# A two-layer hybrid decoder trunk: gathered experts against all experts on TensorE

## The chip, the cores and the metric

The kernel runs on one core of a Trainium2 chip. The metric is device time in microseconds of one execution, as the median of several runs. One execution of the kernel before was also recorded by the hardware profiler; all rows shown here come from it.

## The reference, cut to what matters

256 tokens of width 1024 go through two layers in float32. Layer 0 mixes tokens with a complex diagonal state-space model (S5), a GELU and a gated linear unit; layer 1 with causal attention over three dilated windows (16 heads of 64). After each mixer comes a PEER channel mixer: a retrieval among 16384 single-neuron experts.

```python
def peer_ffn(h, w_q, sub_keys, u_tab, v_tab):        # u_tab, v_tab: (16384, 1024) per layer
    q = (h @ w_q).reshape(bsz, seq, 8, 2, 128)
    s = einsum('blhpe,hpne->blhpn', q, sub_keys)      # 8 heads x 2 halves x 128 keys
    s_top, i_top = top_k(s, 16)
    cand = s_top[..., 0, :, None] + s_top[..., 1, None, :]
    best, pos = top_k(cand, 16)                       # 16 of 256 sums
    idx = first_key * 128 + second_key                # expert number
    gate = softmax(best)
    act = einsum('cd,ckd->ck', h, u_tab[idx])         # 8 x 16 = 128 experts per token
    return einsum('ck,ckd->cd', gate * gelu(act), v_tab[idx])

# layer: x += mixer(rms_norm(x)); x += peer_ffn(rms_norm(x)); at the end rms_norm(x)
# mixer of layer 1: qkv = h @ w_qkv (1024 x 9216), rope, 3 window groups, @ w_o
```

Only 128 of the 16384 experts have a gate that isn't zero for a token, and a gate depends on the expert's first key i and second key j.

## The kernel before, in words

Tokens are two chunks of 128, one token per partition. The work has four phases: layer 0 chunk 0, layer 0 chunk 1, layer 1 chunk 0, layer 1 chunk 1. A phase is a mixer for one chunk, its norms, the query projection (`peer_scores`, L528) and the top 16 (`top_k_part`, L1493, in four quarters of two heads). The experts of one phase are computed under the mixer of the next.

Expert work goes through the class `Gather` (L319). Each phase has 128 steps. At a step GpSimd issues one indirect DMA (L1233) that brings, for 32 tokens x 4 experts, 128 rows of u and v side by side (1 MB) into one of 8 slots of `ringmem`. VectorE multiplies u with the token's h and sums (L1262), ScalarE takes the GELU (L820) and builds a 128 x 32 matrix `S` with the gated activations (L816, L825), and TensorE adds the v rows into the tokens' sums in PSUM banks 0 and 1 (L448), two steps at once. All engines place these steps into their own order of the other work with `g.at(phase, n)`; `QKV_AT`, `HEADS_AT`, `S5_AT` and the like (L343 to L357) say at which pair of steps each part of a mixer comes. `spread_block` (L455) copies h four times for the layout of the gathers; ScalarE also rearranges row numbers and gates (L898).

Weights come over SP's queue in 2 MB items into a double buffer `wt` (L373, L389): GLU, query, Q/K/V and output weights. In layer 1 each chunk reads all 18 items of `w_qkv` for itself. `project` (L505) does 8 matmuls of 512 moving columns for an item (L509); `project_turned` (L513) does 32 of 128 columns (L523), so that the query comes out turned. Each matmul is float32.

Within a phase TensorE, VectorE and ScalarE each run in program order; what they wait for are semaphores counted by item, step and event.

Of the kernel before, what the change touches and what calls it, by code (L numbers as in the profile page):

```python
# [9 lines left out]
U32 = mybir.dt.uint32  # L30
# [4 lines left out]
P = 128  # L35
# [3 lines left out]
KT = D // P  # L39
EPS = 1e-6  # L40
# [12 lines left out]
RING = 8  # L53
PAIRS_G = STEPS // 2
QUAD = 4
TG = P // QUAD
QUADS = STEPS // QUAD
QPQ = QUADS // QUARTERS
# [9 lines left out]
GLU, WQ0, ITEMS0 = 0, 4, 8  # L68
WT0 = 2
QKV, WO, WQ1, ITEMS1 = 0, 18, 20, 24  # L70


C_ID, C_RAMP, C_IOTA, C_COS, C_SIN, C_REP, C_ALL = 0, 128, 256, 272, 400, 528, 656
M_AT = (0, NG * P)
M_ALL = NG * P + NG * 2 * P
A_WORDS = 15872


TopK = namedtuple("TopK", "stop itop itopf best pos posi posj posij posf gsum grec found gex S2 cand eq")


def item(layer, c, i):


    if layer == 0:
        return i - WQ0 if c == 0 else WT0 + i
    return WT0 + ITEMS0 + ITEMS1 * c + i


def norm_event(layer, c, ffn):  # L90

    return 4 * layer + 2 * c + ffn


def build(nc, x, gains, lam, b_in, c_out, d_skip, w_glu, w_qkv, w_o, w_q, keys, experts, consts,
          masks, out):
    ctx = ExitStack()
    with ctx:
# [6 lines left out]

        X = sb("X", [P, NC, D])
        H = sb("H", [P, D])
        Hrep = sb("Hrep", [P, QUAD, D])
        hT = sb("hT", [P, KT, P])
        gT = sb("gT", [P, KT, P])  # L110
        gain = sb("gain", [P, D])
        wt = sb("wt", [P, 2, KT, BLOCK])
        ringmem = sb("ringmem", [P, RING * 2 * D])
        area = sb("area", [P, A_WORDS])
        con = sb("con", [P, C_ALL])
        sel = sb("sel", [P, 2, QSTEPS])
        lay = sb("lay", [P, NC, 2, QUAD, QUADS])
        rows = lay[:, :, 0].bitcast(U32)
        dots = sb("dots", [P, 2, 2])
        gelus = sb("gelus", [P, 2, 2])  # L120
        S = sb("S", [P, 2, 2, TG])
# [15 lines left out]
        rep = con[:, C_REP:C_REP + P]  # L137
        own = con[:, C_REP:C_REP + TG]

# [16 lines left out]
        cosT = view(area, 0, PAIRS, P)  # L156
        sinT = view(area, 4096, PAIRS, P)
        WB = view(area, 8192, KT, 2, P)
        CW = view(area, 10240, PAIRS, 2, 32)
        T1, T2, T3, P1, P2, P3, P4 = [view(area, 12288 + 512 * i, PPT, P) for i in range(7)]  # L160
        mag, z0re, z0im = [zs[:, i, :] for i in range(3)]
        hflat = Hrep[:, :, :].rearrange("p j d -> p (j d)")
        T4 = P1
        MG = [view(area, 12288 + 512 * i, PPT, P) for i in (4, 5)]
        ZR, ZI = [view(hflat, 512 * i, PPT, P) for i in range(2)]
        Q1, Q2, Q3, Q4 = [view(hflat, 2048 + 512 * i, PPT, P) for i in range(4)]
        sig = view(area, 12288, D)

        craw = view(ringmem, 0, 2, PAIRS, GH)
        tmpc = view(ringmem, 1024, 2, PAIRS, GH)  # L170
        small = view(ringmem, 2048, 20, PAIRS)
        wq_ring = [view(ringmem, 4096 * i, KT, BLOCK) for i in (2, 3)]
        wglu = [wt[:, 1]] + [view(ringmem, 4096 * i, KT, BLOCK) for i in (1, 2, 3)]
# [4 lines left out]
        gflat = gT[:, :, :].rearrange("p k t -> p (k t)")  # L178
        keysT = view(area, 12288, HP, NKEYS)
        qT = view(area, 14336, 2, QHP, P)  # L180
        qs = sb("qs", [P, 512])

        def top_k_places(small, big):
            best, pos, posi, posj = [view(small, 192 + 32 * i, QH, TOPK) for i in range(4)]
            return TopK(stop=view(small, 0, QHP, TOPK), itop=view(small, 64, QHP, TOPK).bitcast(U32),
                        itopf=view(small, 128, QHP, TOPK), best=best, pos=pos.bitcast(U32),
                        posi=posi.bitcast(U32), posj=posj.bitcast(U32),
                        posij=view(small, 256, 2, QSTEPS).bitcast(U32),
                        posf=view(small, 320, 2 * QSTEPS), gsum=view(small, 416, QH),
                        grec=view(small, 418, QH), found=view(small, 420, 2, QSTEPS),  # L190
                        gex=view(small, 384, QH, TOPK), S2=view(big, 0, QHP, NKEYS),
                        cand=view(big, 512, QH, TOPK * TOPK), eq=big)

        late = wt[:, 1].rearrange("p k n -> p (k n)")
        late_scores = [view(late, 1024 + 512 * i, QHP, NKEYS) for i in range(2)]
        places = top_k_places(qs, gflat)
        late_places = top_k_places(late[:, 2048:2560], late)

        def top_k_at(ph, i):

            return late_places if ph == 0 and i >= 2 else places

        MS = view(qs, 0, PPT, P)


        K0 = view(area, 0, NG, 8, P)
        V0 = view(area, 3072, NG, D)
        K1 = view(area, 6144, NG, 4, P)
        V1 = view(area, 7680, NG, BLOCK)
        QT = view(area, 9216, NG, 4, P)  # L210
        RA = view(area, 10752, BLOCK)
        RB = view(area, 11264, BLOCK)
        RR = [view(area, 11776 + BLOCK * i, BLOCK) for i in range(2)]
        SS = [view(area, 10752 + 768 * i, 768) for i in range(2)]
        PT = [view(area, 12288 + 768 * i, 768) for i in range(2)]
        mask = view(area, 13824, 2 * NG * P)
# [1545 lines left out]
```

## Time and profile before

| | |
|---|---|
| median of 3 runs | 1752.47 us (1749.7 to 1760.04) |
| span of the profiled execution | 1755.3 us; no other time of it was taken |
| mean granted TensorE clock | 0.868 of full speed |
| PE, PEld busy | 1285.1 us (73%), 544.9 us (31%) |
| DVE, ACT, POOL busy | 1120.6 us (64%), 677.5 us (39%), 616.7 us (35%) |
| moved by DMA | 685.81 MB, mean 391 GB/s |

PE is TensorE's matmuls, PEld its weight loads, DVE VectorE, ACT ScalarE, POOL GpSimd, SP the queue engine. Busy time is the union of the instructions' records. Matmuls are pipelined and their ends are modelled, so the time from one group's start to the next one's is a better price than a record's length. PEclk is the clock that was granted, as a share of 2.4 GHz. "Idle before" names what released an engine that had stood idle.

### The profile page before, as it was taken

The numbers are of one execution on the slowest core, as the hardware profiler recorded it, in microseconds if no ns is written. First come the engines' busy times: TensorE is split into PE (matmuls) and PEld (weight loads), VectorE is DVE, ScalarE is ACT, GpSimd is POOL, SyncE is SP. The second block draws the span as 40 slices with busy tenths as digits, with TensorE's granted clock in tenths as the row PEclk, the third lists the DMA queues.
The fourth block names the chain that finished last, engine by engine and source line by source line (L and its number), as shares of the span: only waits on it lengthen the run. The fifth ranks groups of instructions, "written<-read, shape, count | busy, mean of one in ns | idle before, by whom it ended". The sixth has DMA issues, their size and how long they took to land.

```text
span 1755.3 us, 17565 instructions
## 1 busy us (share of the span) xinstructions
PE 1285.1 (73%) x5714; PEld 544.9 (31%) x5714; DVE 1120.6 (64%) x2526; ACT 677.5 (39%) x2033; POOL 616.7 (35%) x557
## 2 busy tenths in 40 slices
PE   3876565666969968997788895899886975545454
PEld 2463111222713313333244331543451810000000
DVE  8967999863568765436347966553554567676544
ACT  7643232322243257128134333821652233233222
POOL 4213444442242243224223323332442144444442
PEclk9988877688989979998899998999997976786878
DMA  8099999999999999999999999999999899999997
GB/s 332 7 367 378 380 366 390 392 407 422 424 420 423 424 422 421 426 422 421 423 414 418 415 423 411 381 386 424 422 379 423 332 333 411 418 418 412 420 421 299
DMA packets 86636, 685.81 MB, mean 391 GB/s; under 512 B 9872, under 2 KB 10256, under 8 KB 12176
## 3 DMA queue, kind: packets, MB, share of 16 engines
q0 software_dynamic: 73728, 536.90, 74.9%
q1 hardware_dynamic: 12816, 147.79, 20.3%
q8 instruction: 45, 0.74, 0.2%
q14 instruction: 47, 0.39, 0.1%
HBM read 683.60 MB, written 1.05 MB: 390 GB/s over the span
## 4 chain that ended last, share of the span: by engine, by line
PE 34%; DMA 33%; DVE 19%; ACT 6%; issue 5%; POOL 2%; SPq 0%; POOLq 0%; ACTq 0%; DVEq 0%
DMA ringmem<-experts,lay 24%; PE ps L509 11%; PE ps L448 11%; PE ps L523 6%; DMA wt<-w_qkv 6%; DVE ringmem L1262 6%; POOL ringmem L1233 2%; DMA wt<-w_o 2%; ACT S L825 1%; ACT lay L898 1%; PE ps L727 1%; PE ps L702 1%; PE ps L461 1%; PE ps L713 1%; DMA wt<-w_glu 1%
## 5 line engine op out<-in xcount | busy, mean ns | idle before, releaser
L1233 POOL DMA_INDIRECT ringmem<-experts,lay x512 | 585.3, 1143 | 1062.4 <-PE ps L448 932.0
L448 PE MATMUL ps<-ringmem,S 128*32 128x512 f32 x2048 | 618.2, 753 | 368.3 <-ACT S L825 364.3
L1262 DVE CUSTOM_DVE_ANT_0 ringmem<-ringmem,Hrep 128x1024 f32<-128x1024 f32 x384 | 461.1, 1224 | 260.4 <-DMA ringmem<-experts,lay 257.9
L448 PEld LDWEIGHTS ps<-ringmem,S 128*32 128x32 f32 x2048 | 112.6, 126 | 761.7 <-ACT S L825 516.4
L820 ACT ACTIVATE gelus<-dots 128x2 f32<-128x2 f32 x256 | 51.5, 201 | 628.7 <-DVE dots L1262 624.0
L509 PE MATMUL ps<-wt,hT 128*128 128x512 f32 x576 | 256.2, 598 | 13.8 <-DMA wt<-w_qkv 13.8
L1262 DVE CUSTOM_DVE_ANT_0 ringmem<-ringmem,area 128x1024 f32<-128x1024 f32 x128 | 155.6, 1225 | 110.6 <-DMA ringmem<-experts,lay 110.0
L509 PEld LDWEIGHTS ps<-wt,hT 128*128 128x128 f32 x576 | 106.7, 190 | 164.1 <-issue 153.8
L816 ACT ACTIVATE S<-con,lay 128x32 f32<-128x32 f32 x512 | 134.6, 311 | 39.7 <-PE ps L448 39.1
L825 ACT ACTIVATE S<-S,gelus 128x32 f32<-128x32 f32 x512 | 136.8, 314 | 24.6 <-ACT gelus L820 1.1
L523 PEld LDWEIGHTS ps<-hT,wt 128*128 128x128 f32 x896 | 104.4, 197 | 12.1 <-issue 11.9
L523 PE MATMUL ps<-hT,wt 128*128 128x128 f32 x896 | 107.3, 282 | 0.0
L509 PE MATMUL ps<-wt,gT 128*128 128x512 f32 x128 | 63.2, 652 | 12.6 <-DMA wt<-w_o 10.5
L820 ACT ACT_TABLE_LOAD x55 | 70.6, 1283 | 1.0
L898 ACT COPY lay<-sel 32x16 f32<-32x16 f32 (+1 forms) x272 | 54.4, 200 | 18.8 <-DVE sel L1586 15.8
L1090 ACT COPY area<-ps 128x512 f32<-128x512 f32 x12 | 7.0, 586 | 135.3 <-PE ps L509 135.3
L1607 DVE TENSOR_TENSOR area<-ps,con 128x512 f32<-128x512 f32 x24 | 16.6, 690 | 65.9 <-PE ps L509 56.7
L1622 DVE CUSTOM_DVE_ANT_0 area<-ps,area 128x384 f32<-128x384 f32 (+1 forms) x32 | 24.2, 757 | 46.2 <-PE ps L702 46.2
L1510 DVE MAX8 qs<-ps 128x8 f32<-128x128 f32 x56 | 12.6, 285 | 62.0 <-PE ps L546 47.4
L1262 DVE DVE_READ_ACCUMULATOR2_ANT dots<- 128x1 f32 x512 | 42.1, 82 | 0.0
L509 PEld LDWEIGHTS ps<-wt,gT 128*128 128x128 f32 x128 | 26.1, 209 | 50.8 <-issue 34.6
L1065 ACT ACT_TABLE_LOAD x32 | 41.1, 1283 | 0.6
(234 smaller groups left out, 1237.1 us busy)
## 6 DMA issues: line engine op xcount, KB each, us to landing
wt<-w_qkv SPq DMA_DIRECT2D x36, 2048.0 KB, 11.6
wt<-w_q SPq DMA_DIRECT2D x14, 2048.0 KB, 11.3
wt<-w_glu SPq DMA_DIRECT2D x5, 2048.0 KB, 11.9
ringmem<-experts,lay POOLq DMA_INDIRECT x512, 12.5
wt<-w_o SPq DMA_DIRECT2D x4, 2048.0 KB, 14.4
ringmem<-w_glu SPq DMA_DIRECT2D x3, 2048.0 KB, 21.5
gain<-gains SPq DMA_DIRECT2D x9, 512.0 KB, 11.1
area<-keys SPq DMA_DIRECT2D x4, 1024.0 KB, 9.6
```

The lines of the kernel that those rows point to most:

```text
L448: last = pe.matmul(ps[TG * t:TG * (t + 1), half, :], S[:, u % 2, i, :], ring[:, (2 * u + i) % RING, D + half * 512:D + (half + 1) * 512], ...
L461: pe.matmul(ps[:, bank, :], rep[rows_j, :], H[rows_j, half * 512:(half + 1) * 512], start=True, stop=True, skip_group_check=True).then_inc ...
L509: last = pe.matmul(ps[:, bank, :], act[:, k, :], wt[:, n % 2, k, :], start=(k == 0), stop=(k == KT - 1))
L523: last = pe.matmul(ps[:, bank, m * P:(m + 1) * P], w[:, k, m * P:(m + 1) * P], hT[:, k, :], start=(k == 0 and m == parts[0]), stop=(k == K ...
L816: last = act.activation(S[:, u % 2, i, :], own, ACT.Copy, scale=lay[:, phase % NC, 1, j - 1 + i, n:n + 1])
L820: act.activation(gelus[:, u % 2, :], dots[:, u % 2, :], ACT.Gelu_apprx_tanh).then_inc(gelu_ready, 1)
L825: last = act.activation(S[:, u % 2, i, :], S[:, u % 2, i, :], ACT.Copy, scale=gelus[:, u % 2, i:i + 1])
L898: last = act.copy(lay[TG * r:TG * (r + 1), ph % NC, :, j, n:n + width], sel[TG * j:TG * (j + 1), :, at + width * r:at + width * (r + 1)])
L1065: act.activation(SS[u % 2][:, 0:n], SS[u % 2][:, 0:n], ACT.Exp, bias=nmx[:, u:u + 1], scale=DH ** -0.5, accum_out=den[:, u:u + 1]).then_in ...
L1233: pool.indirect_dma_start(ring[:, s % RING, :], None, experts[phase // NC], bass.IndirectOffsetOnAxis(ap=rows[:, phase % NC, j, n:n + 1], ...
L1262: last = v.tensor_tensor_reduce(ring[:, i, 0:D], ring[:, i, 0:D], hrep(phase, j), 1.0, 0.0, ALU.mult, ALU.add, dots[:, b, second:second + 1])
L1622: v.tensor_tensor_reduce(SS[u % 2][:, 0:n], banks(2, 4)[:, at:at + n], mask[:, 0:n], 1.0, NEG, ALU.add, ALU.max, mx[:, u:u + 1]).then_inc( ...
```

## The change

- No gathers. The u and v tables are read whole, in loads of 1 MB: one load holds, for two first keys i, the 128 experts of each. `u_load` multiplies all 128 experts of a first key with the tokens of one chunk (128 columns) or both (256 columns), ScalarE's GELU writes the result to `acts` (seen as `W[second key, chunk, first key, token]`). `v_load` multiplies `W` of one or both chunks with the v rows and adds into PSUM.
- Gates as a matrix. For each token, `second_keys` (VectorE) makes a 128 x 128 matrix with the gate at each chosen expert's second key, one row per chosen expert; `first_keys` (GpSimd) one with a 1 at its first key. TensorE multiplies the two (`gates`), four tokens a group, and `apply_gates` (VectorE) multiplies `W` with the result.
- One stream. SP issues all loads in the order of `stream_order()` into four slots of 1 MB (`RING`), each when the load four before it is used: 448 loads in all. Both chunks share a load of query, Q/K/V and output weights. Chunk two lags: the first `AHEAD` u loads of a layer are used for chunk 0 alone while chunk 1's mixer goes on, and read again for chunk 1; v the same.
- Query projection for both chunks at once (256 columns). Attention's heads run for both chunks after half of the Q/K/V items. GpSimd takes one of four products of chunk 1's scan.

The core of the diff (semaphore and buffer declarations left out; unchanged steps as well):

```diff
-RING = 8
-QUAD = 4
-QKV, WO, WQ1, ITEMS1 = 0, 18, 20, 24
+RING = 4
+LOADS = NKEYS // 2
+LOAD_WORDS = 2 * D
+AHEAD = (34, 30)
+GROUP = 4
+GROUPS_C = P // GROUP
+def stream_order():
+    order = []
+    for layer in range(LAYERS):
+        ahead = AHEAD[layer]
+        if layer == 1:
+            order += [("qkv", t, half) for t in range(QITEMS) for half in range(2)]
+            order += [("wo", i, half) for i in range(2) for half in range(2)]
+            order += [("u", 1, 0, n) for n in range(ahead)]
+        else:
+            order += [("u", 0, 0, n) for n in range(S5_LOADS)]
+            order += [("glu", k) for k in range(KT)]
+            order += [("u", 0, 0, n) for n in range(S5_LOADS, ahead)]
+        order += [("wq", layer, n) for n in range(HP // 2)]
+        order += [("u", layer, 0, n) for n in range(ahead, LOADS)]
+        order += [("u", layer, 1, n) for n in range(ahead)]
+        order += [("v", layer, 0, n) for n in range(LOADS)]
+        order += [("v", layer, 1, n) for n in range(ahead)]
+    return order
+S5_STEP_LOADS = (3, 3, 3, 3, 3, 3, 3, 3)
...
+            for n, key in enumerate(ORDER):
...
+                if n == 0:
+                    sp.wait_ge(cw_ready, 4)
+                if n == 2:
+                    sp.wait_ge(y_ready, KT)
+                    sp.wait_ge(z0_ready, KT)
+                if n >= RING:
+                    sp.wait_ge(used, n - RING + 1)
+                sp.dma_start(ring[:, n % RING, :], source(key)).then_inc(landed[n % RING], 16)
...
+            def u_load(layer, turn_of, n):
+                key = ("u", layer, turn_of, n)
+                at = load(*key)
+                bank = 6 + EVACUATED[key] % 2
+                if EVACUATED[key] >= 2:
+                    pe.wait_ge(evacuated, EVACUATED[key] - 1)
+                alone = turn_of == 1 or n < AHEAD[layer]
+                cols = slice(P * turn_of, P * (turn_of + 1)) if alone else slice(0, SEQ)
+                width = P if alone else SEQ
+                for b in range(2):
+                    for k in range(KT):
+                        last = pe.matmul(ps[:, bank, b * width:(b + 1) * width],
+                                         at[:, D * b + P * k:D * b + P * (k + 1)], hF[:, k, cols],
+                                         start=(k == 0), stop=(k == KT - 1), skip_group_check=True)
+                last.then_inc(used, 1)
+            def v_load(layer, turn_of, n):
+                at = load("v", layer, turn_of, n)
+                chunks = (turn_of,) if turn_of or n < AHEAD[layer] else (0, 1)
+                for b in range(2):
+                    i = 2 * n + b
+                    for c in chunks:
...
+                        for half in range(2):
+                            last = pe.matmul(ps[:, 2 * c + half, :], W[:, c, i, :],
+                                             at[:, D * b + BLOCK * half:D * b + BLOCK * (half + 1)],
+                                             start=first, stop=end, skip_group_check=True)
+                last.then_inc(used, 1)
+            def gates(layer, c, g):
+                q = gate_group(layer, c, g)
+                pe.wait_ge(hot_j_ready, q + 1)
+                pe.wait_ge(hot_i_ready, q + 1)
+                if g >= 2:
+                    pe.wait_ge(gated, q - 1)
+                for r in range(GROUP):
+                    last = pe.matmul(ps[:, 4 + q % 2, r * P:(r + 1) * P], hot_j[q % 2][:, r, :],
+                                     hot_i[q % 2][:, r, :], start=True, stop=True, skip_group_check=True)
+                last.then_inc(gates_done, 1)
+            def experts(layer):
+                ahead = AHEAD[layer]
+                all_scores(layer)
+                for n in range(ahead, LOADS):
+                    u_load(layer, 0, n)
+                turn_sel(layer, 0)
+                for n in range(ahead):
+                    u_load(layer, 1, n)
+                    for g in groups_behind(n, ahead):
+                        gates(layer, 0, g)
+                turn_sel(layer, 1)
+                pe.wait_ge(gated, gate_group(layer, 0, GROUPS_C - 1) + 1)
+                for n in range(ahead):
+                    v_load(layer, 0, n)
+                    for g in groups_behind(n, ahead):
+                        gates(layer, 1, g)
+                pe.wait_ge(gated, gate_group(layer, 1, GROUPS_C - 1) + 1)
+                for n in range(ahead, LOADS):
+                    v_load(layer, 0, n)
...
+            def project(t, c):
...
+                for half in range(2):
+                    w = load("qkv", t, half)
+                    for k in range(4):
+                        last = pe.matmul(ps[:, project_bank(t, c), :], hF[:, 4 * half + k, P * c:P * (c + 1)],
+                                         w[:, BLOCK * k:BLOCK * (k + 1)], start=(half == 0 and k == 0),
+                                         stop=(half == 1 and k == 3), skip_group_check=True)
+                    if c == 1:
+                        last.then_inc(used, 1)
...
+            def first_keys(layer, c):                      # GpSimd
+                for g in range(GROUPS_C):
...
+                    for r in range(GROUP):
+                        last = pool.tensor_scalar(hot_i[q % 2][:, r, :], count, selT[:, c, 0, t:t + 1], None,
+                                                  ALU.is_equal)
+                    last.then_inc(hot_i_ready, 1)
...
+            def second_keys(layer, c, g):                  # VectorE
...
+                for r in range(GROUP):
+                    last = v.tensor_scalar(hot_j[q % 2][:, r, :], count, selT[:, c, 1, t:t + 1],
+                                           selT[:, c, 2, t:t + 1], ALU.is_equal, ALU.mult)
+                last.then_inc(hot_j_ready, 1)
+            def apply_gates(layer, c, g):
...
+                at = W[:, c, :, GROUP * g:GROUP * (g + 1)]
+                v.tensor_tensor(at, at, ps[:, 4 + q % 2, :].rearrange("p (t i) -> p i t", t=GROUP),
+                                ALU.mult).then_inc(gated, 1)
...
-            for s in range(2 * NC * STEPS):
...
-                pool.indirect_dma_start(
-                    ring[:, s % RING, :], None, experts[phase // NC],
-                    bass.IndirectOffsetOnAxis(ap=rows[:, phase % NC, j, n:n + 1], axis=0)
-                ).then_inc(landed[s % RING], 16)
```

## Rows read from the trace of the kernel before

**Rows 1.** The page, busy time of each engine (share of the span), and GB/s in 40 slices:

```profile
PE 1285.1 (73%) x5714; PEld 544.9 (31%) x5714; DVE 1120.6 (64%) x2526; ACT 677.5 (39%) x2033; POOL 616.7 (35%) x557
...
GB/s 332 7 367 378 380 366 390 392 407 422 424 420 423 424 422 421 426 422 421 423 414 418 415 423 411 381 386 424 422 379 423 332 333 411 418 418 412 420 421 299
```

**Rows 2.** The page, DMA queues: packets, MB, share of sixteen engines:

```profile
q0 software_dynamic: 73728, 536.90, 74.9%
q1 hardware_dynamic: 12816, 147.79, 20.3%
```

**Rows 3.** The page, the chain that ended last, by engine and by line:

```profile
PE 34%; DMA 33%; DVE 19%; ACT 6%; issue 5%; POOL 2%; SPq 0%; POOLq 0%; ACTq 0%; DVEq 0%
DMA ringmem<-experts,lay 24%; PE ps L509 11%; PE ps L448 11%; PE ps L523 6%; DMA wt<-w_qkv 6%; DVE ringmem L1262 6%; POOL ringmem L1233 2%; DMA wt<-w_o 2%; ACT S L825 1%; ACT lay L898 1%; PE ps L727 1%; PE ps L702 1%; PE ps L461 1%; PE ps L713 1%; DMA wt<-w_glu 1%
```

**Rows 4.** TensorE's groups by line and form: count, busy us, mean ns, idle before:

```profile
L448 PE MATMUL ps<-ringmem,S 128*32 128x512 f32 x2048 | 618.2, 753 | 368.3 <-ACT S L825 364.3 <-DVE X L1277 3.6
L509 PE MATMUL ps<-wt,hT 128*128 128x512 f32 x576 | 256.2, 598 | 13.8 <-DMA wt<-w_qkv 13.8
```

**Rows 5.** The chain in order of time: start us, us, what:

```profile
456.47 7.34 PE ps L523 x64
...
705.85 7.08 PE ps L509 x16
...
864.52 10.10 PE ps L509 x16
```

**Rows 6.** Stretches: us, busy (instructions) by engine, PEclk, DMA share, GB/s:

```profile
5.00:25.00 20.00, 4.83 (x41) 3.64 (x41) 18.22 (x37) 17.95 (x35) 7.78 (x7) 1.00 1.02 415
456.47:463.81 7.34, 7.34 (x66) 7.34 (x67) 0.00 (x0) 0.58 (x1) 0.55 (x1) 1.00 0.98 413
705.85:712.93 7.08, 7.08 (x18) 2.98 (x20) 2.57 (x5) 1.27 (x5) 2.88 (x2) 1.00 1.03 433
864.52:874.62 10.10, 10.10 (x18) 4.12 (x20) 0.07 (x2) 1.16 (x5) 0.00 (x0) 0.70 1.01 423
```

**Rows 7.** TensorE's other groups by line and form:

```profile
L702 PE MATMUL ps<-area 64*128 64x128 f32 x288 | 41.0, 285 | 0.0
L727 PE MATMUL ps<-area 128*128 128x64 f32 x288 | 36.8, 274 | 0.0
...
L713 PE MATMUL ps<-con,area 128*128 128x128 f32 x144 | 23.3, 292 | 19.8 <-ACT area L1073 19.8
...
L689 PE MATMUL ps<-con,area 128*128 128x128 f32 x96 | 14.6, 275 | 0.0
...
L579 PE MATMUL ps<-Hrep,area 128*32 128x128 f32 x256 | 9.5, 294 | 11.3 <-ACT area L952 11.1 <-DVE Hrep L1434 0.2
L487 PE MATMUL ps<-con,H 128*128 128x128 f32 x48 | 7.3, 300 | 1.3 <-DVE H L1291 1.3
```

**Rows 8.** The chain where chunk one's turned projection starts, and near the end:

```profile
94.30 4.40 PE ps L523 x32
...
1747.79 1.23 DVE X L1277
```

**Rows 9.** ScalarE's, VectorE's and GpSimd's groups by line and form:

```profile
L857 ACT COPY hT<-ps 128x1024 f32<-128x1024 f32 x6 | 6.0, 1002 | 2.3 <-PE ps L487 2.3
...
L1607 DVE TENSOR_TENSOR area<-ps,con 128x512 f32<-128x512 f32 x24 | 16.6, 690 | 65.9 <-PE ps L509 56.7 <-issue 7.4 <-DVE qs L1514 1.0
...
L1510 DVE MAX8 qs<-ps 128x8 f32<-128x128 f32 x56 | 12.6, 285 | 62.0 <-PE ps L546 47.4 <-PE ps L619 14.6
...
L1332 DVE TENSOR_SCALAR area<-area 128x512 f32<-128x512 f32 x1 | 0.4, 426 | 0.0
...
L1166 POOL TENSOR_TENSOR area<-area 128x512 f32<-128x512 f32 x7 | 9.4, 1348 | 26.2 <-DVE Hrep L1434 20.8 <-DVE Hrep L1431 4.8 <-ACT area L927 0.6
L1201 POOL TENSOR_TENSOR zs<-Hrep 128x4 f32<-128x4 f32 x8 | 4.1, 515 | 0.0
```

**Rows 10.** The page, DMA issues: count, KB each, median us to landing:

```profile
wt<-w_o SPq DMA_DIRECT2D x4, 2048.0 KB, 14.4
```

More of the change, by code:

```diff
@@ L82, in item @@
[L82 to L96, printed above, removed]
+ACT_WORDS = NKEYS * P
+A0 = ACT_WORDS
+def stream_order():
[16 more added lines that the diff above has]
+    return order
@@ L210, in build @@
[L210 to L216, printed above, removed]
[L217 to L223 removed]
+        keysT = view(acts, A0, HP, NKEYS)
@@ L483, in turn, with load @@
-            def turn(src, event):
-                pe.wait_ge(normed, event + 1)
-                for k in range(KT):
-                    last = pe.transpose(ps[:, 2 + k // 4, (k % 4) * P:(k % 4 + 1) * P],
-                                        src[:, k * P:(k + 1) * P], ident)
-                last.then_inc(turned, 1)
+            def load(*key):
+                n = AT[key]
+                pe.wait_ge(landed[n % RING], 16 * (n // RING + 1))
+                return ring[:, n % RING, :]
             def turn_halves(src, event, use):
@@ new lines, in wq_load @@
+            def wq_load(layer, n):
+                key = ("wq", layer, n)
+                at = load(*key)
+                pe.wait_ge(evacuated, EVACUATED[key] - 1)
+                for b in range(2):
+                    for k in range(KT):
+                        last = pe.matmul(ps[:, 6 + EVACUATED[key] % 2, b * SEQ:(b + 1) * SEQ],
+                                         at[:, D * b + P * k:D * b + P * (k + 1)], hF[:, k, :],
+                                         start=(k == 0), stop=(k == KT - 1), skip_group_check=True)
+                last.then_inc(used, 1)
@@ L793, in _ @@
+            pe.wait_ge(ramp_in, 16)
+            first_mixer()
+            second_mixer()
+            experts(0)
+            end_of_first()
+            attention()
+            experts(1)
+            for n in range(AHEAD[1]):
+                v_load(1, 1, n)
         @block.scalar
@@ new lines, in gelu_alone, with copy_q @@
+            def gelu_alone(layer, first, end):
+                for n in range(first, end):
+                    gelu_u(layer, 0, n)
+            def copy_q(layer, n):
+                key = ("wq", layer, n)
+                act.wait_ge(used, AT[key] + 1)
+                if n >= 2:
+                    act.wait_ge(scored, HP // 2 * layer + n - 1)
+                act.copy(qT[n % 2].rearrange("p m t -> p (m t)"),
+                         ps[:, 6 + EVACUATED[key] % 2, :]).then_inc(evacuated, 1)
```

1523 lines of the change are left out of this document (686 added, 837 removed).

## The prediction

> **What bounds the kernel now.** I read the page's totals first. The core moves 366 to 424 GB/s in nearly every slice from the third on, while TensorE is busy 73% and VectorE 64% [rows 1]. The queue table says what fills it: the gathers' queue q0 moves 536.90 MB, the weights' q1 147.79, and q0 takes 74.9% of the sixteen engines' time, q1 20.3% [rows 2]. The chain of waits is shared: DMA 33%, PE 34%, VectorE 19%, and its largest line is the landing of gathered expert rows, 24% [rows 3]. So the kernel is bound by its transfers first; TensorE stands close behind, since it does all projections between the gather slots. The question for this change is what happens when the 537 MB go and TensorE gets the experts instead.
>
> **TensorE's price list.** All operands stay float32. The trace writes two records per float32 matmul: 36 projections of 8 matmuls are 576 records of L509 [rows 4]. Sixteen such records (8 matmuls, 512 columns moving) start back to back and take 7.08 us on the chain, so one costs 0.885 us [rows 5]. Sixty-four records of L523 (32 matmuls, 128 columns moving) take 7.34 us: 0.229 us each [rows 5]. In both stretches the granted clock is 1.00, the 2.4 GHz level [rows 6]. At 256 columns there is no row. Twice the 128-column price is 0.459, half the 512-column price 0.4425; I take 0.450, both ends are within 2%. After 16 us of waiting for a DMA the same 16 records took 10.10 us [rows 5], and the clock there was 0.70 in the mean, part of it at the 1.2 GHz level [rows 6]: the full price needs a TensorE that doesn't wait.
>
> **The new expert matmuls.** A load is 1 MB: two first keys, 128 experts each. A u load for one chunk is 2 x 8 matmuls of 128 columns, for both chunks 16 of 256. A v load is 4 matmuls of 512 columns for one chunk, 8 for both. AHEAD = (34, 30) loads per layer serve one chunk alone, twice (once each chunk), and 30 and 34 serve both. Over two layers that is 128 one-chunk and 64 two-chunk loads of u, and the same of v:
> u, one chunk: 2048 x 0.229 = 469 us; u, both: 1024 x 0.450 = 461; v, one chunk: 512 x 0.885 = 453; v, both: 512 x 0.885 = 453. Sum 1836 us.
> This alone is more than the whole kernel now takes. What it replaces on TensorE is the 618 us of L448 [rows 4].
>
> **TensorE's other work after the start.** It is in order and I add it up as one stream, since every part below sits on the same queue:
> - query projections: 2 layers x 8 loads x 16 matmuls of 256 columns = 256 x 0.450 = 115; scores 64 x 0.229 = 15;
> - one-hot gate matmuls: 128 tokens x 2 chunks x 2 layers = 512 x 0.229 = 117 (new);
> - Q, K, V: 288 x 0.885 = 255, the same count as before. "Read once" halves the bytes, not the matmuls. Output projection 28, second chunk's GLU 32 x 0.885 = 28;
> - attention's own matmuls and transposes: 41.0 + 36.8 + 23.3 + 14.6 = 116 [rows 7];
> - second chunk's state-space matmuls: L579 in its dense form 9.5 [rows 7], and the 128 records of L560 at about as much: 19;
> - eight turns of h or o at 7.3 / 6 = 1.2 us, and the turned selections: 12 [rows 7].
> Sum 705 us.
>
> **Before and behind it.** The first chunk's mixer is unchanged in its chain, so TensorE's first turned projection at 94.30 us [rows 8] is where the first u load starts. I let nothing of those 94 us be saved. The end is as now: add, norm and output, from 1747.8 to 1755.3, 7.5 us [rows 8]; chunk one's output has gone long before.
>
> **What TensorE still waits for.** Some seventeen handovers are exposed: five of the turned h through ScalarE (1.0 us copy [rows 9]), four where a v stretch waits for the last gated group (one 0.69 us multiply and its semaphores [rows 9]), two per layer round the scores, the starts and ends of the two attention halves, the turned selections. At about 1.5 us each, an estimate from those rows, 25 us. From below it is 10 us, from above 60.
>
> Total 94 + 1836 + 705 + 25 + 7.5 = 2668 us of span.
>
> **Why the rest is covered.**
> - Transfers. There are 212 + 236 = 448 loads, 470 MB, with start-up, keys, gains and masks about 488 MB. One-chunk loads are the fastest consumers: 3.54 us (v) or 3.67 us (u) per 1.05 MB, so 296 GB/s are needed. In 5 to 25 us, where only SP's queue ran, it moved 415 GB/s [rows 6]. With four slots a load may be in flight for three loads' work, 10.6 us. Without that cover: if a load took the 14.4 us of w_o [rows 10], a 2 MB transfer amid gathers, a one-chunk load would cost 4.8 us instead of 3.6.
> - SP is in order; its gain, key and mask loads wait for norms, y or o that TensorE's stream has passed by then, since loads are issued at most four ahead.
> - ScalarE's GELU of a load: 256 or 512 PSUM columns. Even its copy of 1024 PSUM columns takes 1.0 us [rows 9]; TensorE spends 3.7 or 7.2 us on the load.
> - VectorE's top-16: a quarter is 20 searches of 128 words at 0.285 [rows 9], 10 of 256 words at some 0.42, passes over 3500 words at 0.69 per 512 [rows 9] and a dozen small ones, an estimate of 17 us; 136 us a layer, beside 216 or 245 us of two-chunk u loads and most of the query projections.
> - Gates. Per group of four tokens VectorE makes four 128-word multiplies (at most the 0.43 us of 512 words [rows 9], at least a third of that) and one gate multiply with a strided PSUM read: 0.69 us as contiguous, perhaps four times that. 1.3 to 4.5 us, taken as 1.6. GpSimd makes four 128-word compares. Its rows have 4 words at 0.52 us and 512 words at 1.35 [rows 9]: 2.1 to 5.4 us a group, taken as 2.6 by the nearer end. A group is given one load and its four gate matmuls: 3.6 + 0.9 = 4.5 us. Only the far ends fill it.
> - The state-space steps of chunk two: VectorE needs nine passes over 512 words at 0.69 [rows 9], two scans at about twice that and small ones, some 9.5 us a step; TensorE has three u loads, 11.0 us, plus its own 2.4.
>
> **The rivals.**
> 1. Gates bind. The mask making on GpSimd, or VectorE's strided multiply, needs 5.4 us a group where TensorE offers 4.5. 128 groups x 0.9 = 115 us more: 2780. For it: GpSimd's 1.35 us row [rows 9]. Against: the operations are a quarter of that size. 8%.
> 2. The ring starves TensorE. 1 MB loads land in 14.4 us: 256 one-chunk loads x 1.2 = 307 us more, 2970, and with it the clock would fall to the lower level in the waits. For it: w_o's row. Against: 415 GB/s with no gathers. 5%.
> 3. TensorE streams faster than its rows. Then it isn't the bound, and the transfers are: 488 MB at 415 GB/s are 1176 us, plus some 75 us of the start in which the ring can't be filled: 1250, faster than now. It decides from the point where the 2541 us of matmuls shrink to some 1630, 0.57 us for 512 columns. For it: matmul ends in the trace are modelled. Against: the starts of 16 records 7.1 us apart, over and over, with DMA at 433 GB/s beside them [rows 6]. 1%.
> The Trainium skill, "TensorE: Matmul & The Clock Gate", section "Back-to-back issue gap", speaks for rival 3: it gives a sustained 131 ns for a matmul of 512 columns among weight loads, where this trace has 442 ns per record. By the page's figure twice 131 ns would make an expert matmul 0.26 us and that rival true; the trace disagrees.
> 4. Attention or handovers cost more: the second half's heads run as a chain through three engines and not as TensorE's stream, or the clock does not stay up in one-chunk stretches. 60 to 110 us more: 2750. 12%.
> My forecast, TensorE's stream nearly without gaps: 74%.
>
> **How the numbers follow.** The sum is made against the profiled execution, whose span was 1755.3 us; the median of the runs is 1752.5, a factor 0.998, so 2668 becomes 2663. Own range of the forecast: 10 us of handovers instead of 25 and the cheaper 256-column price give 2640; all matmuls 1% cheaper 2615; 60 us of handovers give 2700. Rivals 1 and 4 reach to 2780, which leaves rival 2 above and rival 3 below, about 8% with the tails. Range 2610 to 2785. A measurement of this kernel tells about 0.5% from no change. Faster by over 0.5%: only rival 3, 1%. Within 0.5%: nothing lands there, 1% for what I haven't seen. Slower: 98%.
>
> **What would show it.** TensorE busy 94% or more of the span from 95 us on, its clock near 1.00 there; the two v lines together near 906 us, u near 930, gates near 117, Q, K, V near 255. DMA some 488 MB and under 190 GB/s over the span. Waits of TensorE on landed loads in the tens of microseconds at most; if they are hundreds, rival 2. Waits on the masks of GpSimd or VectorE in every group: rival 1. If 16 records of 512 columns take clearly under 7 us, the price list and with it the whole prediction is wrong.

## The result and the profile after

The changed kernel takes 2606.71 us (median of 4 runs, 2605.67 to 2607.88) where the kernel before takes 1756.26 (4 runs on the same chip): the ratio is 1.4858, 95% interval 1.4805 to 1.491. The prediction was 2663 us in a range of 2610 to 2785, so direction and mechanism came out as forecast, and the time 2% lower, 3 us under the range's low end.

The page of the changed kernel: busy time of each engine, the granted clock in 40 slices (tenths), what the queues moved, and the chain of waits by engine and by line.

```profile
PE 2536.8 (97%) x12318; PEld 1769.7 (68%) x12318; DVE 753.6 (29%) x2104; ACT 312.7 (12%) x560; POOL 348.0 (13%) x565
...
PEclk9899999999999999999999879999999999999999
...
DMA packets 67810, 489.42 MB, mean 188 GB/s; under 512 B 7776, under 2 KB 8032, under 8 KB 9440
...
q1 hardware_dynamic: 67680, 487.55, 52.9%
...
PE 96%; DVE 3%; issue 1%; ACT 1%; DMA 0%; POOL 0%; DVEq 0%
PE ps L448 35%; PE ps L467 34%; PE ps L677 10%; PE ps L521 4%; PE ps L478 4%; PE ps L706 2%; PE ps L729 1%; PE ps L762 1%; PE ps L652 1%; PE ps L717 1%; PE ps L491 1%; PE ps L692 0%; PE ps L578 0%; DVE ring L1371 0%; PE ps L599 0%
```

Against [rows 1 to 3] everything has moved to one engine. TensorE went from 73% of a short span to 97% of a long one, and its share of the chain from 34% to 96%. The queue of the gathers (536.90 MB) has gone, 685 MB in all have become 489, and DMA has no place left on the chain. The bytes did go down as the change says; nothing was waiting for them any more.

TensorE's groups by line and form (count of records, two to a float32 matmul; busy us, mean ns; idle before and its releaser):

```profile
L467 PE MATMUL ps<-ring,acts 128*128 128x512 f32 x2048 | 889.9, 592 | 1.6 <-DVE acts L1519 1.6
L448 PE MATMUL ps<-hF,ring 128*128 128x128 f32 x4096 | 475.4, 277 | 1.8 <-ACT hF L830 1.1 <-ACT hF L837 0.7
L448 PE MATMUL ps<-hF,ring 128*128 128x256 f32 x2048 | 442.4, 379 | 0.0
L677 PE MATMUL ps<-ring,hF 128*128 128x512 f32 x576 | 256.4, 600 | 1.1 <-ACT hF L830 1.1
L521 PE MATMUL ps<-onehot 128*128 128x128 f32 x1024 | 134.5, 275 | 0.0
L478 PE MATMUL ps<-hF,ring 128*128 128x256 f32 x512 | 112.9, 379 | 1.1 <-ACT hF L830 1.1
```

The counts are those of the prediction; 889.9 + 475.4 + 442.4 = 1808 us of expert matmuls stand where L448 of before had 618 [rows 4]. The idle columns hold 1 to 2 us: TensorE's whole list of waits has no transfer in it, and the stretches say the same. From 92.6 us, 2.6 us before the first u matmul, to the last matmul:

```profile
92.60:1230.00 1137.40, 1123.00 (x5629) 794.33 (x5630) 343.17 (x959) 101.70 (x184) 167.34 (x264) 0.99 0.58 204
1230.00:1640.00 410.00, 403.46 (x1822) 268.73 (x1821) 79.33 (x192) 76.02 (x149) 0.00 (x0) 0.93 0.35 122
1640.00:2598.40 958.40, 956.66 (x4398) 676.51 (x4396) 244.51 (x815) 69.63 (x120) 149.24 (x256) 1.00 0.56 198
```

(us, busy time with instructions of TensorE, its weight loads, VectorE, ScalarE, GpSimd; granted clock, DMA share, GB/s.) In 2505.8 us TensorE is idle for 22.7. Only attention, the middle row, runs at a mean clock of 0.93. It has one long stretch at half the clock, the 1.2 GHz level, although TensorE is hardly idle there. The last of the 512-column projection matmuls started at 1473.3 us; from then on it ran the short ones of attention, and at 1480.3 us the clock fell:

```profile
1480.30:1534.90 54.60, 53.88 (x234) 49.54 (x232) 11.22 (x38) 16.74 (x37) 0.00 (x0) 0.50 0.00 1
```

The masks and gates are hidden. The page's rows of them, and the landing of the loads:

```profile
L1188 POOL TENSOR_SCALAR onehot<-con,selT 128x128 f32<-128x128 f32 x512 | 298.7, 601 | 1755.3 <-ACT selT L877 1514.1
...
L1519 DVE TENSOR_TENSOR acts<-acts,ps 128x512 f32<-128x512 f32 x128 | 87.9, 687 | 315.7 <-PE ps L521 315.7
L1508 DVE TENSOR_SCALAR onehot<-con,selT 128x128 f32<-128x128 f32 x512 | 166.1, 384 | 14.6 <-ACT selT L877 14.5
...
ring<-u_tab SPq DMA_DIRECT2D x192, 1024.0 KB, 4.8
ring<-v_tab SPq DMA_DIRECT2D x192, 1024.0 KB, 4.7
```

A group of four tokens costs GpSimd 4 x 0.601 = 2.40 us and VectorE 4 x 0.384 + 0.687 = 2.22, while TensorE offers 4.3 to 4.5. A load lands 4.7 or 4.8 us after its issue, not after the 14.4 of [rows 10].

Last, the price of a matmul, from the chain in order of time (start us, us, what):

```profile
333.31 207.20 PE ps L448 x960
540.84 7.15 PE ps L448 x64
...
2261.58 336.75 PE ps L467 x784
```

The first is 480 matmuls of 256 columns: 207.20 / 480 = 0.4317 us each. The second, 32 of 128 columns: 0.2234. The last, 392 of 512 columns: 0.859. The prediction had 0.450, 0.229 and 0.885.

### The profile page after: what moved, and what is told of

Same layout as the page of the kernel before. It is cut to its first block, busy times and chain, and to the rows that moved or that the text cites. A ratio compares the mean times of both kernels' runs of the same rounds, so it can differ in the third digit from the quotient of the medians.

```text
span 2605.9 us, 29080 instructions
## 1 busy us (share of the span) xinstructions
PE 2536.8 (97%) x12318; PEld 1769.7 (68%) x12318; DVE 753.6 (29%) x2104; ACT 312.7 (12%) x560; POOL 348.0 (13%) x565
## 3 DMA queue, kind: packets, MB, share of 16 engines
HBM read 486.47 MB, written 1.05 MB: 187 GB/s over the span
## 4 chain that ended last, share of the span: by engine, by line
PE 96%; DVE 3%; issue 1%; ACT 1%; DMA 0%; POOL 0%; DVEq 0%
PE ps L448 35%; PE ps L467 34%; PE ps L677 10%; PE ps L521 4%; PE ps L478 4%; PE ps L706 2%; PE ps L729 1%; PE ps L762 1%; PE ps L652 1%; PE ps L717 1%; PE ps L491 1%; PE ps L692 0%; PE ps L578 0%; DVE ring L1371 0%; PE ps L599 0%
## 5 line engine op out<-in xcount | busy, mean ns | idle before, releaser
L448 PE MATMUL ps<-hF,ring 128*128 128x128 f32 (+1 forms) x6144 | 917.8, 311 | 1.8 <-ACT hF L830 1.1
L448 PEld LDWEIGHTS ps<-hF,ring 128*128 128x128 f32 x6144 | 857.2, 192 | 56.7 <-ACT hF L830 1.3
L467 PE MATMUL ps<-ring,acts 128*128 128x512 f32 x2048 | 889.9, 592 | 1.6 <-DVE acts L1519 1.6
L467 PEld LDWEIGHTS ps<-ring,acts 128*128 128x128 f32 x2048 | 384.4, 190 | 460.4 <-issue 458.5
L1188 POOL TENSOR_SCALAR onehot<-con,selT 128x128 f32<-128x128 f32 x512 | 298.7, 601 | 1755.3 <-ACT selT L877 1514.1
L677 PE MATMUL ps<-ring,hF 128*128 128x512 f32 x576 | 256.4, 600 | 1.1 <-ACT hF L830 1.1
L1508 DVE TENSOR_SCALAR onehot<-con,selT 128x128 f32<-128x128 f32 x512 | 166.1, 384 | 14.6 <-ACT selT L877 14.5
L521 PEld LDWEIGHTS ps<-onehot 128*128 128x128 f32 x1024 | 129.0, 192 | 29.7 <-issue 28.9
L521 PE MATMUL ps<-onehot 128*128 128x128 f32 x1024 | 134.5, 275 | 0.0
L478 PE MATMUL ps<-hF,ring 128*128 128x256 f32 x512 | 112.9, 379 | 1.1 <-ACT hF L830 1.1
L478 PEld LDWEIGHTS ps<-hF,ring 128*128 128x128 f32 x512 | 96.3, 190 | 13.8 <-ACT hF L830 1.3
L706 PE MATMUL ps<-acts 64*128 64x128 f32 x288 | 51.5, 334 | 0.7 <-DVE mx L1565 0.7
L706 PEld LDWEIGHTS ps<-acts 64*128 64x128 f32 x288 | 44.2, 233 | 5.2 <-issue 1.7
```

The costliest lines, as they stand in the source:

```text
L448: last = pe.matmul(ps[:, bank, b * width:(b + 1) * width], at[:, D * b + P * k:D * b + P * (k + 1)], hF[:, k, cols], start=(k == 0), stop= ...
L467: last = pe.matmul(ps[:, 2 * c + half, :], W[:, c, i, :], at[:, D * b + BLOCK * half:D * b + BLOCK * (half + 1)], start=first, stop=end, s ...
L478: last = pe.matmul(ps[:, 6 + EVACUATED[key] % 2, b * SEQ:(b + 1) * SEQ], at[:, D * b + P * k:D * b + P * (k + 1)], hF[:, k, :], start=(k = ...
L521: last = pe.matmul(ps[:, 4 + q % 2, r * P:(r + 1) * P], hot_j[q % 2][:, r, :], hot_i[q % 2][:, r, :], start=True, stop=True, skip_group_ch ...
L677: last = pe.matmul(ps[:, project_bank(t, c), :], hF[:, 4 * half + k, P * c:P * (c + 1)], w[:, BLOCK * k:BLOCK * (k + 1)], start=(half == 0 ...
L706: last = pe.matmul(ps[:, at // 512, at % 512:at % 512 + P], Qt[half][c][rows, gr, h // 2, :], Kt[half][kb][rows, gr, h // 2, :], start=Tru ...
```

## Experiments

Ten kernels were run. The first four are one run each, beside one of the kernel before (1753.03 us), and are compared with the 2606.71 us of the changed kernel; so is the half-product kernel further down.

**Is a gate matmul on the path?** Of the four gate products of a group only one is made; masks and multiplies stay. The output lacks the other tokens' gates.

```
-                for r in range(GROUP):
+                for r in range(1):
```

> The changed kernel with one of the four gate matmuls of each group of tokens; the other three are left out, so three of four tokens get wrong gates. All one-hot rows are still made, all gates still applied. Theory A (TensorE's in-order stream is the whole time, nothing else is near it): 3 x 128 matmuls of 128 columns less, at the 0.2234 us that lie between starts in the changed kernel's trace: 86 us less, 2521 us. Rival B (the stretch of gates runs at the pace of the makers of the masks, GpSimd or VectorE): under 20 us less, 2590 or more.

Measured: 2522.62 us, 84 less. 384 matmuls have gone, 0.219 us each, nearly the full 0.2234 from start to start: theory A. The gates lie on TensorE's stream, and the masks that still were made did not hold it up.

**How much cover do the loads need?** A u or v load is issued only when the load two before it is used, in place of four.

```
-                    sp.wait_ge(used, n - RING + 1)
+                    sp.wait_ge(used, n - (2 if key[0] in "uv" else RING) + 1)
```

> The changed kernel, but a u or v load is issued only when the load two before it is used, not four before. Bytes and TensorE's work are the same. Theory A with landings as the trace has them (4.7 to 4.8 us from issue): a one-chunk load gives only 3.4 to 3.6 us of cover, so 256 of them wait 1.2 to 1.4 us each: 310 to 360 us more, about 2940; two-chunk loads (6.9 us) wait for nothing. With four in flight transfers then cost nothing because of their depth. Rival B (only bandwidth counts, 296 GB/s are needed and 415 are there): no change, 2606. Rival C (TensorE's clock falls in such short waits as well): 3000 or more, granted clock under 0.9.

Measured: 2721.6 us, 115 more: between theory A's 310 to 360 and rival B's nothing. The granted clock stays at 0.983, so rival C is out. TensorE's waits in this run (total us, times, longest), and its timeline in the last stretch:

```profile
PE ps L467 <- DMA ring<-v_tab: 46.9, 45, 2.3
PE ps L448 <- DMA ring<-u_tab: 33.7, 46, 1.7
```

```profile
2647.68 7.25 PE L467 MATMUL ps<-ring,acts 128*128 128x512 f32 x16 [1.35 <-DMA ring<-v_tab]
2656.26 7.24 PE L467 MATMUL ps<-ring,acts 128*128 128x512 f32 x16 [1.33 <-DMA ring<-v_tab]
```

Sixteen records are two loads, so one wait of 1.35 us falls on every second load: two loads land together and their slots come free one after the other. The loads for two chunks don't wait, and those with gates behind them hardly do (some 10 of the 81 us). So transfers are hidden in the changed kernel, but by the depth of the ring: with half of it the one-chunk loads without gates cost 0.86 us more each (7.25 + 1.35 for two, against 6.87). Theory A's mistake was a wait for each of 256 loads: 128 of them have gates behind them, and of the others every second one waits.

**What does a change of the stationary width cost?** The starts of the records in the trace of before gave the suspicion: within a projection they are 0.429 us apart, but 0.523 and 0.533 us where L448's 32-column stationary has just been in use. Two kernels add 128 matmuls of 128 columns among the second chunk's u loads, one with a stationary of 32 columns, one with 128; their results are not used.

```
+                    if turn_of == 1:
+                        pe.matmul(ps[0:32, 0, 0:P], hF[:, b, 0:32], hF[:, b, 0:P],
+                                  start=True, stop=True, skip_group_check=True)
```

(and `ps[0:128, ...], hF[:, b, 0:128]` in the other.)

> The changed kernel with 128 extra matmuls that nobody reads: after each first key of a one-chunk u load of chunk two, one of 128 moving columns whose stationary part is 32 columns wide. Theory A (a change between 32 and 128 stationary columns costs TensorE about 0.2 us in all, which is what my prices of groups contained): 128 x (0.22 + 0.2) = 54 us more, 2660. Rival B (the 0.2 us came with waits on semaphores at the groups' borders and not with the width): 128 x 0.22 = 29 us more, 2635.

> The same 128 extra matmuls at the same places, but with 128 stationary columns, as their neighbours have. Theory A and rival B alike: 128 x 0.2234 = 29 us more, 2635. It is the yardstick for the narrow ones: the difference of the two is the price of the change of width, 25 us by theory A and 0 by rival B.

Measured: 2676.29 us with the narrow one, 2635.66 with the wide one. The wide matmul costs 29 / 128 = 0.226 us, its list price. The difference of the two is 40.6 us for 128 changes there and back, 0.32 us each, so the cause is theory A's and the price higher than its 0.2. The timelines show where it goes (start us, us, what), first the narrow kernel, then the wide one, last the kernel before:

```profile
545.45 2.05 PE L448 MATMUL ps<-hF,ring 128*128 128x128 f32 x16
547.43 0.41 PE L452 MATMUL ps<-hF 128*32 128x128 f32 x2
547.76 2.05 PE L448 MATMUL ps<-hF,ring 128*128 128x128 f32 x16
```

```profile
545.88 1.95 PE L448 MATMUL ps<-hF,ring 128*128 128x128 f32 x16
547.66 0.39 PE L452 MATMUL ps<-hF 128*128 128x128 f32 x2
547.89 1.06 PE L524 MATMUL ps<-onehot 128*128 128x128 f32 x8
```

```profile
703.94 1.91 PE L448 MATMUL ps<-ringmem,S 128*32 128x512 f32 x8
705.78 7.13 PE L509 MATMUL ps<-wt,hT 128*128 128x512 f32 x16
712.84 1.91 PE L448 MATMUL ps<-ringmem,S 128*32 128x512 f32 x8
```

From the narrow matmul to the next group it takes 0.33 us where the wide one takes 0.23, and the sixteen records before the narrow one take 1.98 us where the others take 1.78. Record by record, the four steps round each narrow matmul last 205, 133, 202 and 213 ns, and every step round the wide one 112, also at the borders where a new load or a group of gates begins: rival B, a cost of the borders, is out. Over all 128 places these steps make 39 of the 40.6 us, so the difference isn't a difference between two single runs. The kernel before has the same pattern: 523 ns into the projection, 533 after its first record, 523 back into L448, where 429 is usual. A piece of the chain that holds sixteen records holds two of these steps, 0.2 us.

**Is it the matmuls' length, and what comes next?** The expert matmuls read only the upper 16 bits of each operand, as bfloat16, in one pass; nothing else is changed.

```
+            def upper(ap):
+                return ap.bitcast(mybir.dt.bfloat16)[:, 1::2]
-                                         at[:, D * b + P * k:D * b + P * (k + 1)], hF[:, k, cols],
+                                         upper(at[:, D * b + P * k:D * b + P * (k + 1)]), upper(hF[:, k, cols]),
```

(and the same for `W` and `at` in `v_load`.)

> The expert matmuls (u and v, 5,120 in all) read only the upper 16 bits of each operand as bfloat16, so that TensorE needs one pass; every load, wait, mask and gate stays as it is, and the rest stays fp32. The products are of truncated operands. Theory A (TensorE's time in the expert matmuls sets the time, and transfers are the next bound): the 1,808 us of expert matmuls fall to what the 384 loads of 1 MB take. At the 422 to 424 GB/s of the slices of before that is 2.47 us each, 950 us, if the one-pass matmuls are shorter than that everywhere: 2607 - 1808 + 950 = about 1750 us. If one pass costs half of the fp32 time, the 128 loads for both chunks stay TensorE's at 3.45 us and the sum is 1808 -> 441 + 632 = 1073, about 1870 us. TensorE then waits for the ring in the expert stretches. Theory B (a fixed cost of the order: waits between engines, buffers, masks; not the length of the matmuls): it stays above 2400 us. Theory C (masks and gates become the bound in the 128 loads with gates): these stay at 4.5 us each and it comes to 2000 us or more.

Measured: 1737.55 us (4 runs, 1736.49 to 1740.41), 0.9917 of the kernel before, interval 0.9887 to 0.9946. 869 us have gone, and theory A's 1750 holds: TensorE now waits for loads, 152 us in all, and 63 us for ScalarE's GELU of u results. (The expectation's count of 5,120 expert matmuls is wrong, they are 4,096; its sum goes by the 1,808 us and not by the count.)

```profile
L471 PE MATMUL ps<-ring,acts 128*128 128x512 bf16 x1024 | 298.3, 428 | 107.1 <-DMA ring<-v_tab 105.9 <-DVE acts L1523 0.8
```

```profile
602.06 1.99 PE L471 MATMUL ps<-ring,acts 128*128 128x512 bf16 x8 [0.51 <-DMA ring<-v_tab]
604.55 1.98 PE L471 MATMUL ps<-ring,acts 128*128 128x512 bf16 x8 [0.51 <-DMA ring<-v_tab]
607.03 1.98 PE L471 MATMUL ps<-ring,acts 128*128 128x512 bf16 x8 [0.51 <-DMA ring<-v_tab]
```

```profile
560.00:680.00 120.00, 89.06 (x367) 34.75 (x366) 13.44 (x30) 1.22 (x2) 10.18 (x18) 0.94 1.01 419
```

The timeline (start us, us) has a two-chunk v load every 2.48 us, which is 1.05 MB at 423 GB/s, the transfers' rate, where the float32 kernel needs 6.87 us; the stretch shows a DMA share of 1.01.

**The same question in float32.** Half of the v products are left out: of the two key rows in a load only the first is multiplied.

```
+                        if b == 1 and not end:
+                            continue
```

> Of the two key rows in each v load the second is left out of the product (its 512-column matmuls aren't issued, save in the last load of a chain): about 1,024 of the 2,048 expert v matmuls at 0.8585 us go, fp32 stays, all loads stay. Theory A with a floor of the transfers (2.47 us for 1 MB at 424 GB/s): the 64 loads for both chunks fall from 6.87 to 3.43 (-220 us), the 64 with gates behind them by 1.72 (-110 us; 2.6 us are left, just above the floor), the 64 of the second chunk alone from 3.43 to 2.47 only (-61 us): -391 us, 2216 us. Theory A without such a floor: -1024 x 0.8585 = -879 / ... of which each left-out matmul saves its full 0.8585 us, -440 us for the one-chunk loads and the rest in proportion: 2607 - 879 = 1728 us if 1,024 matmuls go; the loads decide between them, since the trace shows how long each kind takes. Theory B (the v stretches are bound by something else than matmuls): no change, 2607 us.

Measured: 2225.18 us, 382 less. The expectation took the 2,048 records for matmuls; there are 1,024, and 504 were left out. At 0.859 us each, without a floor, they are 433 us, 2174; with the floor of 2.47 us for a load it expected 2216. The chain of waits shows the floor in the second chunk's loads: its DMA pieces start 9.8 to 9.9 us apart, and since a slot is filled again when the load four before is used, that is four loads of about 2.48 us:

```profile
890.13 7.70 DMA ring<-v_tab
...
899.90 7.87 DMA ring<-v_tab
...
909.82 7.88 DMA ring<-v_tab
```

**A version faster than both.** Gate products, Q, K, V and output projections and chunk two's GLU also read the upper halves (`upper(...)` around both operands, as above).

> As the run with one-pass expert matmuls, and now the gate products, the Q, K and V projections, the output projection and chunk two's GLU also read only the upper 16 bits. Theory A (what is left is TensorE's fp32 outside the experts, and transfers inside them): in the stretches with gates the DMA share is 0.97 already, so the 512 gate matmuls bring at most 20 us; the 288 projection matmuls fall from 0.8585 to about 0.29 us (298.3 us of busy time over 1,024 one-pass matmuls) and are then bound by their 36 loads (2.5 us each, 90 us): -157 us at the most; GLU and output projection -20 us. In the second half of the projections attention's own chain of ScalarE and VectorE takes part of it back. 1737 - 177 + 40 to 90 = 1600 to 1650 us. Theory B (attention's chain or the loads already set the time there): 1700 us or more.

Measured: 1545.31 us (4 runs, 1539.33 to 1552.3), 0.8798 of the kernel before (0.8769 to 0.8827); 55 us better than theory A's best: the 192 us gained are more than the 177 it gave as the most. The projections, from the first matmul to the last, shrank from 314 us to 149, 165 less where it gave 157 at the most, although attention's first heads lie between them: its chain took nothing back there. TensorE's waits and its chain by engine:

```profile
PE ps L471 <- DMA ring<-v_tab: 124.5, 169, 1.4
PE ps L452 <- DMA ring<-u_tab: 75.1, 87, 2.1
PE ps L452 <- ACT acts L857: 63.3, 15, 5.8
PE ps L525 <- DVE onehot L1514: 47.3, 34, 18.3
```

```profile
DMA 40%; PE 32%; DVE 23%; issue 2%; ACT 1%; POOL 1%; DVEq 0%
```

The transfers now hold the largest share of the chain, but ScalarE's GELU and VectorE's masks make TensorE wait as well; the projections wait 15.0 us in all for their loads. Like every one-pass version here it multiplies operands cut to their upper 16 bits.

**Control: would one pass have helped the kernel before?** Its 1,024 v products of gathered rows read the upper halves.

> The kernel before with the v products of its gathered experts in one pass (1,024 of its matmuls of 512 columns read the upper 16 bits), nothing else changed. Theory A (in its gather stretches the transfers are the bound, DMA share 0.97 to 1.01): TensorE's shorter products buy little, 1735 to 1755 us, though 10.7% of the chain lies on them. Theory B (TensorE's link in the ring of buffers counts): half of these 188 us goes, 1660 us.

Measured: 1769.36 us (3 runs), 1.0087 of the kernel before (1.0063 to 1.0112): not faster, and outside theory A's span on the slow side. TensorE's busy time in them fell from 618 us [rows 4] to 235, and its mean granted clock from 0.868 to 0.687; the matmuls that did not change took longer:

```profile
L513 PE MATMUL ps<-wt,hT 128*128 128x512 f32 x576 | 283.9, 650 | 47.5 <-DMA wt<-w_qkv 45.9 <-issue 1.6
L452 PE MATMUL ps<-ringmem,S 128*32 128x512 bf16 x1024 | 235.2, 553 | 572.3 <-ACT S L829 563.6 <-DVE X L1281 4.8 <-issue 3.4
...
L706 PE MATMUL ps<-area 64*128 64x128 f32 x288 | 72.9, 434 | 0.1
L731 PE MATMUL ps<-area 128*128 128x64 f32 x288 | 63.0, 400 | 0.0
```

The attention lines were 41.0 and 36.8 us in [rows 7]. So shorter expert products buy the kernel before nothing; what is seen is a lower clock. That this loss is the whole of the 14 to 15 us is an inference. A kernel before whose projections take one pass as well was not run.

**What is "weights read once" worth?** Q, K and V weights are loaded once for each chunk again.

```
-            order += [("qkv", t, half) for t in range(QITEMS) for half in range(2)]
+            order += [(("qkv0", "qkv")[c], t, half) for t, c in QKV_RUNS for half in range(2)]
...
-                    if c == 1:
-                        last.then_inc(used, 1)
-                if c == 0:
-                    last.then_inc(first_projected, 1)
+                    last.then_inc(used, 1)
```

(ScalarE and VectorE then wait on `used` for chunk one, too.)

> The changed kernel in fp32 with one part undone: each Q, K, V weight is loaded once for each chunk again, 36 more loads of 1 MB (37.7 MB). Theory A (TensorE's stream is the bound): a projection takes 6.87 us and its two loads 4.9 us at 424 GB/s, so it is hidden: 2607 us, at most 10 more at the start of the projections. Theory B (transfers are part of the bound there): 36 loads x 2.47 us, 2696 us.

> The same undoing in the kernel with one-pass experts, gates and projections. Theory A: with short matmuls the 72 loads of the projections need 178 us at 2.47 us each, where they now run in 149 us (723.6 to 872.3 us of the span) with attention's first heads among them: 30 to 50 us more than 1545, 1575 to 1595 us; reading once pays only here. Theory B (hidden as in fp32, behind attention's heads): 1545 to 1555 us.

Measured: in float32 2614.18 us (2 runs, 2607.19 and 2621.17), 7 us over the changed kernel with its two runs 14 us apart, so no difference that this can tell, and no wait of TensorE for a Q, K or V weight. With one-pass matmuls 1590.39 us (2 runs, 1584.93 and 1595.86), 45 us more than with the weights read once; the wait for them rises from the 15.0 us of that kernel to

```profile
PE ps L683 <- DMA ring<-w_qkv: 42.4, 40, 2.3
```

This part of the change is worth nothing where TensorE's stream is the bound, and 45 us where transfers count.

## Where the prediction was right, and the term that was mis-sized

- **The bound.** "TensorE's stream nearly without gaps" held: 97% busy, 22.7 us idle from 92.6 us to the last matmul. The one-pass kernel is the proof by removal: with the matmuls shorter and every wait kept, 869 us go.
- **The counts.** 4,096 expert matmuls, 512 gate products, 288 projections: all as worked out. The gates are on the stream at their full price, as counted (384 of them, 84 us).
- **The price list was wrong, and it carries the term that missed.** The expert matmuls were put at 1836 us. By the starts on the chain they take 2048 x 0.2234 + 1024 x 0.4317 + 1024 x 0.859 = 1779 us, 57 less; the same prices take 16 off the 705 us of the other work. The step that failed is "so one costs 0.885 us": the 7.08 us of sixteen records [rows 5] hold some 0.2 us besides 16 x 0.429 = 6.87, since in the kernel before a projection stands between matmuls of L448, whose stationary is 32 columns wide. The 64 records are 7.15 us at the clean price; of the 0.19 us more, 0.10 is one such step, and the rest comes from the ends of the chain's piece, which don't fall on starts of records. The pair of kernels with narrow and wide matmuls in between shows this toll, 0.32 us there and back. All expert and gate matmuls of the changed kernel are 128 wide and among themselves don't pay it. Dividing a short group's time by its count put a part of a fixed cost on each of 4,096 matmuls. The prediction had named its own sign of this, sixteen records in clearly under 7 us: they take 6.87.
- **The same step set the range too narrow.** Its low end allowed "all matmuls 1% cheaper"; they were 2.4% to 4% cheaper. The time lies only 3 us below that end because attention's clock took back a part.
- **Attention** cost more than in the kernel before. The forecast took 116 us, the busy times of [rows 7]; their records overlap. From each record's start to the next one's, the same four lines are 106 us before and 123 after. The increase lies where the clock was halved, 1480.3 to 1534.9 us: a group of twelve records of L706 takes 1.60 us ahead of it and 2.93 in it, and the attention matmuls in this stretch take 54 us, where the prices of those ahead of it give 29.

```profile
1401.90 1.60 PE L706 MATMUL ps<-acts 64*128 64x128 f32 x12
...
1502.16 2.93 PE L706 MATMUL ps<-acts 64*128 64x128 f32 x12
```

  This is the kind of cost that rival 4 named, far below its 60 to 110 us. Why the clock fell there, no run settles.
- **The sum again, from the starts in the trace:** 95 + 1785 for the experts + 696 for the other work + 22 of handovers + 7.5 = 2606 us, the span. The forecast of 2668 was 62 too high: 51 in the experts (the clean prices give 57, the one-chunk u loads took 6 back), 16 in the prices of the other work and 3 in the handovers, less 7 for attention and 1 at the start.
- **The factor 0.998** was the wrong way round: the profiled execution took 2607.65 us, 1.8 us over its span. It made 5 us.
- **Handovers, tail, start:** 22, 7.5 and 95.2 us (the first u matmul) against 25, 7.5 and 94.
- **Rival 1 (gates bind)** was off: 2.40 us on GpSimd against the 2.6 taken, 2.22 on VectorE against 1.3 to 4.5. **Rival 2 (ring starves)** was off, as loads land in 4.7 us; the run with half the depth shows that starving begins there, at 115 us. **Rival 3** was false in float32, yet it named the next bound rightly: with one pass the kernel ran into the transfers, at 1738 us and not its 1250, since only the expert part got shorter.
- The page "TensorE: Matmul & The Clock Gate" of the Trainium skill, section "Back-to-back issue gap", has 131 ns for 512 columns in a sustained stream; records here start 429 ns apart in float32, and about 225 ns apart in the one-pass kernel at a granted clock of 1.00 (600 to 612 us). Neither reaches the page's figure. The section's other figure, some 216 ns for one matmul by itself, is near the 225 of the stream.

## What to carry to other kernels

Replacing gathers by dense products trades bytes for TensorE time, so price the products first: here 196 MB less cost 1,190 us more of float32 matmuls, and only with one pass per matmul did the dense form win. With the expert products alone in one pass, the two forms stand at 1737.55 (dense) and 1769.36 us (gathered), each 1% or less from the kernel before. The 0.88 is not the dense form's alone: 165 of its last 192 us come from one-pass projections, and gathers with these weren't tried. All of it costs precision, as the operands are cut to 16 bits. Take the price of a matmul from the distance of starts in a long run of the same shape, not from a short group divided by its count. A saving in bytes shows only in the version where transfers bind: the same "read once" was worth nothing in one kernel and 45 us in the other.

## What the runs showed of the hardware

- Changing the stationary operand between 128 columns and 32 cost 0.32 us there and back, spread over four steps between records (205, 133, 202, 213 ns where 112 are usual).
- In the kernel before, the v products of two steps, with 32 stationary columns each, go to different partitions of PSUM, and their records start in pairs 7 ns apart. Four such matmuls of 512 columns (eight records) take 1.84 us from start to start, 703.94 to 705.78; with 128 stationary columns four take 4 x 0.859 = 3.44.
- A bfloat16 matmul can read the upper halves of float32 words in place, for both operands, with no conversion by another engine: 512 columns start about 225 ns apart, against 2 x 429 ns in float32, so one pass was nearly four times as fast.
- Less TensorE work did not bring less time: with its v products in one pass the kernel before took 1769 us against 1755, its granted clock fell from 0.868 to 0.687, and unchanged attention matmuls were busy 1.7 to 1.8 times as long. In the changed kernel the clock halved for 55 us in which TensorE was busy 53.9 us, with attention's short matmuls alone.
- A `tensor_scalar` of 128 words takes 601 ns on GpSimd (a compare) and 384 ns on VectorE (a compare and a multiply).
